# Two accumulating transfers issued later, and one copy moved ahead of a weight split, in a two-layer encoder trunk

## What is computed

```python
h = _rmsnorm(x, g_ffn[l])
z = _dwconv_centred(h @ w_up[l], conv_w[l], conv_b[l])   # 1024 -> 2 * 2816, then 3 taps along the tokens
z_gate, z_val = jnp.split(z, [D_FF], axis=-1)
x = x + (jax.nn.silu(z_gate) * z_val) @ w_down[l]        # 2816 -> 1024
```

## Time and profile before

| | us |
|---|---|
| median of 3 runs | 1074.29 (1073.46 to 1074.56) |
| the profiled execution: its own time | 1073.97 |
| its span, first to last instruction | 1072.1 |
| TensorE busy | 1061.3 (99% of the span) |
| GpSimd busy | 720.4 |
| ScalarE busy | 598.6 |
| VectorE busy | 584.5 |

### The profile page before, as it was taken

The page is one execution under the profiler, slowest core; times in us unless marked ns, Lnnn a source line. Parts: engine busy times, 40 slices in busy tenths (PEclk is TensorE's granted clock), DMA queues, the critical chain, the costliest instruction groups (busy, mean ns, idle before and its releaser), DMA issues.

```text
span 1072.1 us, 19199 instructions
## 1 busy us (share of the span) xinstructions
PE 1061.3 (99%) x6924; PEld 954.8 (89%) x6924; DVE 584.5 (55%) x922; ACT 598.6 (56%) x844; POOL 720.4 (67%) x388
## 2 busy tenths in 40 slices
PE   9999999999999999999999999999999999999997
PEld 7788888998899989998878888889989998899987
DVE  4735754576156730776636358446651776136654
ACT  8835447775366623775548344576744775157641
POOL 5343238996999857995534323589969995699940
PEclk9999999999999999999999999999999999999999
DMA  8332136686898757872622221568769975689502
GB/s 304 102 98 80 60 138 157 190 184 198 203 226 202 215 150 168 212 168 91 182 76 88 79 80 60 181 133 220 199 161 256 209 175 180 171 190 238 150 20 79
DMA packets 49780, 168.09 MB, mean 157 GB/s; under 512 B 5776, under 2 KB 8592, under 8 KB 49680
## 3 DMA queue, kind: packets, MB, share of 16 engines
q1 hardware_dynamic: 36304, 119.61, 34.8%
q0 software_dynamic: 12672, 46.14, 23.4%
q10 hardware_dynamic: 704, 1.07, 0.3%
HBM read 141.64 MB, written 2.10 MB: 134 GB/s over the span
## 4 chain that ended last, share of the span: by engine, by line
PE 92%; POOL 3%; DVE 2%; ACT 1%; issue 1%; DMA 1%; SPq 0%; DVEq 0%; ACTq 0%
PE acc L1736 13%; PE acc L2022 13%; PE acc L2025 13%; PE acc L2024 13%; PE acc L1737 13%; PE acc L1738 13%; PE acc L1863 3%; PE acc L1865 3%; PE acc L1864 3%; POOL w_lo L591 2%; DVE arena L1543 1%; PE sides L1833 1%; PE sides L1935 1%; PE sides L1951 1%; DMA x<-xT 1%
## 5 line engine op out<-in xcount | busy, mean ns | idle before, releaser
L591 POOL TENSOR_TENSOR w_lo<-w_raw,w_hi 128x1024 fp32r<-128x1024 f32 x108 | 277.1, 2684 | 47.2 <-ACT w_hi L982 31.3
L601 POOL TENSOR_TENSOR w_lo<-w_raw,w_hi 128x1024 fp32r<-128x1024 f32 x52 | 125.2, 2414 | 202.0 <-ACT w_hi L717 202.0
L2022 PE MATMUL acc<-xg_hi,w_hi 128*128 128x256 f32 x688 | 195.6, 284 | 0.1
L2024 PE MATMUL acc<-xg_lo,w_hi 128*128 128x256 f32 x688 | 194.7, 283 | 0.0
L2025 PE MATMUL acc<-xg_hi,w_lo 128*128 128x256 f32 x688 | 194.7, 283 | 0.0
L1736 PE MATMUL acc<-feat_hi,w_hi 128*128 128x512 f32 (+1 forms) x484 | 185.3, 383 | 1.0 <-DVE feat_lo L1479 1.0
L1737 PE MATMUL acc<-feat_lo,w_hi 128*128 128x512 f32 (+1 forms) x484 | 185.0, 382 | 0.0
L1738 PE MATMUL acc<-feat_hi,w_lo 128*128 128x512 f32 (+1 forms) x484 | 184.9, 382 | 0.0
L2022 PE MATMUL acc<-t_hi,w_hi 128*128 128x256 f32 x528 | 149.9, 284 | 1.8 <-POOL w_lo L591 1.4
L2024 PE MATMUL acc<-t_lo,w_hi 128*128 128x256 f32 x528 | 149.4, 283 | 0.0
L2025 PE MATMUL acc<-t_hi,w_lo 128*128 128x256 f32 x528 | 149.4, 283 | 0.0
(11 more groups left out here) (196 smaller groups left out, 2133.7 us busy)
## 6 DMA issues: line engine op xcount, KB each, us to landing
w_raw<-slabs SPq DMA_DIRECT2D x144, 512.0 KB, 4.3
arena<-slabs SPq DMA_DIRECT2D x32, 512.0 KB, 4.4
mixer_sb<-slabs SPq DMA_DIRECT2D x26, 512.0 KB, 5.5
arena<-slabs POOLq DMA_DIRECT2D x24, 512.0 KB, 5.7
w_raw<-slabs POOLq DMA_DIRECT2D x20, 512.0 KB, 5.7
second_s<-slabs SPq DMA_DIRECT2D x12, 512.0 KB, 5.2
second_s<-arena POOLq DMA_DIRECT2D x12, 512.0 KB, 7.6
mixer_sb<-w_raw POOLq DMA_DIRECT2D x10, 512.0 KB, 7.5
```

Of the source, the lines that this page charges most:

```text
L591: pool.tensor_tensor(lo, source, hi.bitcast(F32), ALU.subtract).then_inc(lo_done, counted(unit))
L601: pool.tensor_tensor(w_lo[:, w], w_raw[:, w], w_hi[:, w].bitcast(F32), ALU.subtract).then_inc(lo_done, 1)
L2022: pe.matmul(out, wh, xh, start=(first and k == 0 and r == 0), stop=False, skip_group_check=True)
L2024: pe.matmul(out, wh, xl, start=False, stop=False, skip_group_check=True)
```

## The change

On GpSimd, the third quad's (quad 2's) two sums are issued later, in the turn of quad 1 alone. `add_s1(L, 2)` stood after the low part of S1 and now stands after that of S2. `add_s2(L, 2)` stood after the low part of S2 and now stands after that of S3. All other quads keep their order. On ScalarE, the copy of U2 of quad 0 and the high part of S1 of quad 1 change places.

```diff
             def low_quad(L, q, following):
                 low_of_quad(L, q, S1_)
-                if following:
+                if following and q > 1:
                     add_s1(L, q + 1)
                 low_of_quad(L, q, A11_)
                 add_s3(L, q)
                 low_of_quad(L, q, A12_)
                 add_s4(L, q)
                 low_of_quad(L, q, S2_)
-                if following:
+                if following and q > 1:
                     add_s2(L, q + 1)
+                elif following:
+                    add_s1(L, q + 1)
                 low_of_quad(L, q, A22_)
                 low_of_quad(L, q, S3_)
+                if following and q == 1:
+                    add_s2(L, q + 1)
                 low_of_quad(L, q, S4_)
...
                 high_s3(0)
+                copy(0, S2_, 1, u2_copy)
                 high_s1(1)
-                copy(0, S2_, 1, u2_copy)
                 copy(0, S1_, 3, p5_copy)
```

## The result

The changed kernel is slower: 1078.40 us median of 12 runs (1077.42 to 1080.33), beside 1075.21 us (12 runs, 1073.46 to 1077.70) for the kernel before in the same measurement. The ratio is 1.0031, 95% interval 1.0020 to 1.0042. The profiled execution took 1078.62 us, with a span of 1076.7; before it was 1073.97 and 1072.1. The forecast was +1.1 us; the loss is 3.2 us between the medians and 4.6 us between the two spans.

A forecast was written before the change was run, and what follows sets the result against it. TensorE, busy 1061.3 of 1072.1 us, bounds the kernel. Per layer, -0.07 us left from earlier low parts plus 0.63 from waiting gave +0.56, +1.1 for both: 1075.4 us from 1074.29. Range 1073.4 to 1077.0.

The forecast's parts named there:

- What t will be: Time t from issue to landing of quad 2's `add_s1` transfer, beside SyncE's load: taken as 6.3 us.
- the twin: Old-trace issue at 371.6 with a load 0.2 us behind it, taken as nearest likeness; its transfer took 7.0 us.
- the prediction's formula: Change for both layers from GpSimd's wait at `add_s2`: 2 x (t - 5.74) us, with a floor of -0.14.
- The wake-up: Delay at `add_s2` between the awaited sum's landing and GpSimd going on: costed at 0.29 us.
- e: Lateness of S4's low part in quad 1 from waiting at `add_s2`: t - 5.67, forecast 0.63 us a layer.
- late-landing rival: `add_s1` shares DMA engines with SyncE's load, lands late, GpSimd stands at `add_s2`: +3.5 us at t = 7.5; chance 0.15.
- The copy's stop: TensorE's stop of 0.46 us before S3 of quad 0 goes; GpSimd's low part of S1 starts 0.48 later.
- A11 of quad 1: TensorE arrives early and meets a new stop of about 0.2 us, released by VectorE; about 0.1 us gain survives.
- S2 and A22 of quad 1: TensorE's starts and stops there come 0.42 us earlier, since the low parts before them end earlier.
- S2 of quad 2: TensorE gets a new stop at about 242.0 us, released by a low part; without waiting, 0.07 of 0.42 us is left.
- The rule that spoke against a wait: Skill page's 2.0 us plus bytes over 436 GB/s: 3.2 us landing, GpSimd never waits at `add_s2`, sum -0.14 us.
- a landing between 5.7 and 6.8 us: The forecast case for `add_s1` of quad 2, with GpSimd waiting at `add_s2`; chance 0.60.

The follow-up runs named there:

- e4: The changed kernel, with SyncE's load beside the first quad-2 sum waiting one low part longer (A22 of quad 1); 1076.04 us, ratio 0.9998 to the kernel before.
- e1: The kernel before with only the copy of U2 moved ahead of the high part of S1 of quad 1; 1077.04 us, ratio 1.0006.
- e6: The kernel before with quad 2's `add_s2` after S3's low part and `add_s1` after A11's, just ahead of `add_s3`; 1074.48 us, ratio 0.9988.
- e8: Repeat of e6: the kernel before with `add_s1` just ahead of `add_s3` and `add_s2` after S3's low part; 1074.18 us, ratio 0.9984.
- e7: The kernel before with `add_s3` and `add_s1` beside `add_s4` after A12's low part, and `add_s2` after S3's; 1082.90 us, ratio 1.0060.
- e9: The changed kernel measured again on the same chip; 1079.55 us, ratio 1.0036 to the kernel before.

## Why the prediction was wrong

*The step that failed is "What t will be".* The transfer was taken at 6.3 us, halfway between the undisturbed 5.6 and the twin's 7.0. It took 7.27 us in layer 0 (220.91 to 228.18) and 7.36 in layer 1 (748.38 to 755.74). Halving had no ground: the load ran for its whole length within the sum's time, as it did at the twin, and e4 shows that without it t is 5.39 and 5.80. The prediction had the row of the right neighbour and then moved away from it towards a case that lacked its condition. It had a second such row: at this very place, with this very load half a microsecond behind, the sum of S2 had taken 7.3 us before, though it adds from SBUF and not from HBM. Part of the size came from how an issue is recorded. One that stands right behind a low part starts in the record some 0.3 us before GpSimd is free (1.19 us long here, 0.87 at the twin). Counted from the end of the issue the landings are 6.08 and 6.16 us after it, and the twin's is 6.13 (7.0 less 0.87). Taken whole, in this way, the twin would have given t = 7.3 and, by the prediction's formula, +3.1 us.

*The wake-up was mis-sized too.* It was put at 0.29 us from the wait before line 650 and measured 0.56: the sum landed at 228.18, and the issue is recorded at 228.74, in layer 1 at 755.74 and 756.30.

*The rest of the sum holds.* With t and the wake-up as measured, e is 1.60 + 0.27 and the layer 1.87 - 0.07 = 1.80 us, measured 1.83. In layer 1 it is 1.69 + 0.27 - 0.07 = 1.89, measured 1.89. The mechanism, a wait at `add_s2` for a sum that the load beside it slows, was forecast; its size was that of the late-landing rival, which the prediction gave 0.15 and 1077.8 us at t = 7.5.

*The copy's stop* was right: it is gone, and S1's low part is 0.48 us later. e1 prices that move at +0.5 us a layer, since without the `add_s1` edit nothing pays it back.

*A11 of quad 1* was nearly right: a long step of 0.27 us with no idle time shown, where a stop of about 0.2 was forecast, at 214.90 and so 0.05 after the end of VectorE's line 1533 (the 1529 of the earlier trace rows). From ScalarE's start A11 comes 0.16 us earlier than before, so of the 0.46 us of the copy's stop no more than that lives past this point.

*S2 and A22 of quad 1* start 13.80 and 17.09 us after ScalarE's start; S2 did so after 14.16 before. That is 0.36 us earlier, with 0.42 forecast. The trace credits this stop in layer 0 to ScalarE's copy, not to the low part.

*S2 of quad 2* was right in kind: a stop that was not there before, 0.29 idle, at 244.16. From ScalarE's start that is 36.55 us, where it was 34.78, so the 1.77 us of delay are in it. The larger part of it is already lost at S4 of quad 1, which the prediction called only possible: with a wait of 1.8 us GpSimd's delay outruns TensorE before quad 2.

*The rule that spoke against a wait* did not hold. No accumulating transfer of 512 KB from HBM landed sooner than 5.1 us in any run here, and none from SBUF to SBUF sooner than 4.5 (line 644); the sum awaited at `add_s2` took 7.3. The Trainium skill, page "DMA: Bandwidth & Descriptors", section "Anatomy of one DMA — SWDGE (gpsimd) path", puts a DMA issued by GpSimd at about 2.0 us plus the bytes over 436 GB/s, an estimate of 3.2 us for this one. By that there would have been no wait; the landings measured here differ from it, and they decide.

The range ended at 7.1 us for t. The chance of 0.60 for a landing between 5.7 and 6.8 us rested on the same halving. The medians' 3.2 us is less than the 3.7 us of both stretches; an estimate of why, from the table, is that a collision adds some 0.4 us to a stretch of the kernel before and nothing to one of the changed kernel. What no run isolates is which share of the 1.6 to 1.9 us comes from the load's reads and which from its writes.

## What to carry to other kernels

When an issue is moved to a new place, list the transfers that will start within its length, find the landing that had the same company in the old trace, and take that one whole: the company sets the time, not the mean over the line. Read an issue's end as the start of the clock, since the recorded start shifts with what stands ahead of it. A good place for an issue is one where its engine waits anyway (e6, by its stretches), and far enough ahead of its user to hold the slowest landing seen, not the median.

## What the hardware showed that was not expected

**VectorE and GpSimd collide in a near tie.** Ahead of the stretch, VectorE makes `t_lo` by four subtractions in each layer, while GpSimd makes low parts. VectorE's second subtraction in the kernel before and in e8:

```profile
176.52 0.96 DVE L1474 SCALAR_TENSOR_TENSOR t_lo<-arena,t_hi 128x768 fp32r<-128x768 f32 x1 [2.20 <-ACT t_hi L961]
```

```profile
176.74 3.88 DVE L1478 SCALAR_TENSOR_TENSOR t_lo<-arena,t_hi 128x768 fp32r<-128x768 f32 x1 [2.20 <-ACT t_hi L965]
```

GpSimd's low part starts 0.53 us behind the first of these (177.05) and 0.35 behind the second:

```profile
177.09 2.70 POOL L591 TENSOR_TENSOR w_lo<-w_raw,w_hi 128x1024 fp32r<-128x1024 f32 x1
```

The same VectorE instruction takes 0.96 or 3.88 us, and in the second case it ends 0.8 us after GpSimd's. The 11 profiles have 22 such layers. Where GpSimd's low part is recorded at most 0.48 us behind, the subtraction took 3.9 to 4.0 us (8 layers); from 0.51 us on it took 0.96 (14 layers). What moves GpSimd is its wait at line 650 for the sum of S2 of quad 0. In three of the 14 layers that sum landed after 8.0 to 8.1 us, where it took 6.7 to 7.1 in all others. One of the three is layer 0 of the changed kernel:

```profile
177.59 0.88 POOL L650 DMA_DIRECT2D w_raw<-second_s  x1 [2.01 <-DMA second_s<-arena]
```

These 11 layers, the 8 and the 3, are late at VectorE's third subtraction, and in them alone it is slow as well. Before, and in the changed kernel:

```profile
194.00 0.95 DVE L1474 SCALAR_TENSOR_TENSOR t_lo<-arena,t_hi 128x768 fp32r<-128x768 f32 x1
```

```profile
194.87 3.84 DVE L1478 SCALAR_TENSOR_TENSOR t_lo<-arena,t_hi 128x768 fp32r<-128x768 f32 x1
```

```profile
195.19 2.70 POOL L591 TENSOR_TENSOR w_lo<-arena,w_hi 128x1024 fp32r<-128x1024 f32 x1
198.85 0.74 POOL L611 TENSOR_TENSOR mixer_sb<-arena 128x256 f32<-128x256 f32 x1 [0.97 <-DVE t_lo L1478]
```

GpSimd was 1.0 us late when its low part began (195.19, 194.16 before), by the late landing. Its wait for VectorE makes that 1.7 us (198.85, 197.17 before), and TensorE stops for a low part at 204.47, 0.68 us idle. The stretch starts 0.9 us later in the three layers and 1.6 to 1.8 in the eight. That goes with the spread of about 4 us between runs of one kernel, and with e6 and e8, one kernel with spans of 1070.7 and 1075.4. It lies ahead of the changed code; that no edit here shifts its odds was argued from the place and not tested. Why the sum at line 650 lands sooner or later stays open.

The Trainium skill, page "SBUF — State Buffer", section "Who interferes with whom", has a VectorE instruction with two SBUF inputs contend with a GpSimd instruction that reads SBUF. The trace agrees that one of the two is held: VectorE by 2.9 us (3.84 against 0.95), or else GpSimd by 0.3 (its low part took 3.04 beside the short subtraction at 194.00, and 2.70 here). The same section of the Trainium skill says that the order of issue decides who is blocked. At the third subtraction VectorE's record starts first in every layer, by 0.13 to 0.24 us where it is short and by 0.16 to 0.35 where it is long, so the records do not show that order there.

**TensorE's clock fell at two stops.** In layer 0 of e7 the granted clock is 0.99 in the window of the stop and 0.50 in the next (1.2 of 2.4 GHz). Between the matmul of 228.07 and that of 231.53 TensorE had none. From 234 to 240 it is 0.69 on average, and from 240 to 246 it is 1.00 again. In layer 1 TensorE stopped for 3.01 us, and the clock fell there too (0.62 from 762 to 768). In no other profile here did TensorE stop for longer than 1.6 us (e9) before its last matmul, and in none did the clock fall before that.
